# First block's output projection: from float32 products, one token tile after another, to float32r parts, half of the inner dimension at a time over all tokens

## The chip, the cores and the metric

One Trainium2 chip, one core of it. The metric is the device time of one execution of the whole program in microseconds (us), the median of repeated runs. Before the change it is 3400.55 us (three runs, 3399.44 to 3404.88).

## The reference, cut to what matters

The program is two blocks over 1024 tokens of width 1024: a state-space block, then a block with attentions and a mixture of experts. The change is in the seam between them. What is computed there, in the terms of the reference:

```python
# end of the first block: x_mix is (1024 tokens, D_INNER = 2048)
x = x + gate[:, None] * (x_mix @ w_out[i])          # w_out: 2048 x 1024
x1 = rmsnorm(x, final_norm_w)
# start of the second block
h = rmsnorm_2(x1, norm1_g[l]) * (1.0 + sc1) + sh1
proj = jnp.matmul(h, w_in[l])
```

## The kernel before, in words

`attentions` (L1838) opens a stage with `rows`, five rows of 1024 numbers broadcast over the 128 partitions (gate, final norm weight, the second block's gain and shift, and a scratch row). `second_input` (L1831) allocates `hh` and `hl` (tiles p_high and p_low), the two float32r parts of the transposed `h` that the second block's projection reads, and calls `close_first` (L1220) and then `project_second` (L1479). A float32r part pair is made so: ScalarE copies a float32 value to float32r (the high part), VectorE subtracts that from the value (the low part), and TensorE adds three products, high by high, high by low and low by high (`three`, L132).

`close_first` does not use such parts for its own product. All 16 inner slices of `w_out` (2048 x 1024, 8 MB) are brought as float32 into one tile c_w by four DMAs of 2 MB on GpSimd's queue (L1322). Then, for each tile t of 128 tokens (eight of them, `for t in range(NT)`, L1331):

- `sync(t)` (L1240) brings 128 rows of the mixer's output (2048 columns, 1 MB) into c_mix on SyncE's queue.
- `tensor_turn` (L1251) transposes them on TensorE, four 128x128 blocks a quarter, four quarters a tile, and `scalar_turn` (L1262) copies each quarter from PSUM to c_mT on ScalarE.
- `tensor(t, quarters)` (L1269) multiplies: 16 inner slices by 2 halves of 512 columns, 32 float32 products a tile, recorded through the helper `products` (L125, matmul at L128).
- `close(t)` (L1283), on VectorE: times gate (L1287), plus x (L1290), the norm's sum of squares (`Norm.rstd`, L1208), a square root on ScalarE (L1214), a reciprocal (L1216), times final norm weight giving x1 (L1295), which SyncE stores (L1297); then again a norm (L1299), gain (L1302) and shift (L1304), giving h.
- `turn_h(t)` (L1306) transposes h on TensorE in two halves (helper `turns`, L136, matmul at L138), ScalarE makes the high part (L1317), VectorE the low part (L1319).

The order on each engine is the order in which the program calls these: `tensor(t, (0, 1))`, `turn_h(t - 1)`, `tensor(t, (2,))`, two quarters of the next tile's transposes, `tensor(t, (3,))`, the other two, `close(t)`. The stage ends when all its signals have arrived; then `project_second` brings its weights (L1514), splits them into parts (L1524, L1526) and multiplies.

Of the kernel before, what the change touches and what calls it, by code (L numbers as in the profile page):

```python
# [66 lines left out]
class Stage:  # L67
# [5 lines left out]

    def sb(self, name, shape, dt=F32):
        return self.stack.enter_context(self.core.nc.sbuf_tensor(name, shape, dt))

    def sem(self, name, unit=1):
        s = self.core.nc.alloc_semaphore(name)
# [23 lines left out]
def row(ap):  # L102
    return ap.partition_broadcast(P)
# [17 lines left out]
def flat2(ap):  # L121
    return ap.rearrange("p a n -> p (a n)")
# [13 lines left out]
def turns(pe, pairs, ident):  # L136
    for o, a in pairs:
        last = pe.transpose(o, a, ident)  # L138
    return last
# [1077 lines left out]
        dve.wait_ge(*vec.now())  # L1217


def close_first(core, dram, tables, hh, hl, rows):  # L1220

    pe, dve, act, pool, sp = core.pe, core.dve, core.act, core.pool, core.sp
    ident = tables["mats"][:, C_ID, :]
    eps = tables["eps"][:, 0:1]
    with Stage(core) as s:
        KM = 2 * D // P
# [5 lines left out]
        w_in, rows_in = [s.dma(f"w_out_in{j}") for j in range(4)], s.dma("c_rows_in")  # L1232
        mix_in, x_in, turned, copied = s.pair("c_mix_in"), s.dma("c_x_in"), s.sem("c_turned"), s.sem("c_copied")
        summed, gated, added, vec, rooted = (s.sem("c_" + k) for k in ("summed", "gated", "added", "vec", "rooted"))
# [3 lines left out]
        m2 = dram["mod2"][0, :]  # L1238

        def sync(t):  # L1240
            b, at = t % 2, slice(P * t, P * t + P)
            if t >= 2:
                sp.wait_ge(*turned.at(4 * t - 4))
            sp.dma_start(mix[b][:], dram["mix"][at, :]).then_inc(*mix_in[b].up())

        def sync_x(t):
            if t:
                sp.wait_ge(*added.at(t))
            sp.dma_start(x[:], dram["x"][P * t:P * t + P, :]).then_inc(*x_in.up())

        def tensor_turn(t, quarters):  # L1251
            b = t % 2
            if quarters[0] == 0:
                pe.wait_ge(*mix_in[b].at(t // 2 + 1))
            for q in quarters:
                n = 4 * t + q
                if n >= 2:
                    pe.wait_ge(*copied.at(n - 1))
                turns(pe, [(core.bank[:, 4 + q % 2, 128 * j:128 * j + 128], mix[b][:, 512 * q + 128 * j:512 * q + 128 * j + 128])
                           for j in range(4)], ident).then_inc(*turned.up())  # L1260

        def scalar_turn(t, quarters):  # L1262
            if t >= 2:
                act.wait_ge(*summed.at(t - 1))
            for q in quarters:
                act.wait_ge(*turned.at(4 * t + q + 1))
                act.activation(mT[t % 2][:, 4 * q:4 * q + 4, :], core.bank[:, 4 + q % 2, :].rearrange("p (j n) -> p j n", j=4), ACT.Copy).then_inc(*copied.up())

        def tensor(t, quarters):  # L1269
            b = t % 2  # L1270
            if t >= 2:
                pe.wait_ge(*gated.at(t - 1))
            for q in quarters:
                if t == 0:
                    pe.wait_ge(*w_in[q].at(1))
                pe.wait_ge(*copied.at(4 * t + q + 1))
                for half in range(2):
                    last = products(pe, core.bank[:, 2 * b + half, :], [(mT[b][:, k, :], w[:, k, 512 * half:512 * half + 512])
                                                                        for k in range(4 * q, 4 * q + 4)], start=q == 0, stop=q == 3)
            if quarters[-1] == 3:  # L1280
                last.then_inc(*summed.up())

        def close(t):  # L1283
            b, at = t % 2, slice(P * t, P * t + P)
            dve.wait_ge(*summed.at(t + 1))
            dve.wait_ge(*vec.now())
            dve.tensor_tensor(y[:], flat2(core.bank[:, 2 * b:2 * b + 2, :]), gate, ALU.mult).then_inc(*gated.up())  # L1287
            dve.wait_ge(*gated.at(t + 1))
            dve.wait_ge(*x_in.at(t + 1))
            dve.tensor_tensor(y[:], y[:], x[:], ALU.add).then_inc(*added.up())  # L1290
            dve.wait_ge(*added.at(t + 1))
            norm.rstd(y[:], eps)
            if t:
                dve.wait_ge(*x1_stored.at(t))
            dve.scalar_tensor_tensor(out=x1[:], in0=y[:], scalar=norm.rs[:, 0:1], in1=fin, op0=ALU.mult, op1=ALU.mult).then_inc(*x1_done.up())  # L1295
            sp.wait_ge(*x1_done.at(t + 1))
            sp.dma_start(dram["x1"][at, :], x1[:]).then_inc(*x1_stored.up())  # L1297
            dve.wait_ge(*x1_done.at(t + 1))
            norm.rstd(x1[:], eps)  # L1299
            if t:  # L1300
                dve.wait_ge(*h_turned.at(2 * t))
            dve.scalar_tensor_tensor(out=h[:], in0=x1[:], scalar=norm.rs[:, 0:1], in1=gain, op0=ALU.mult, op1=ALU.mult).then_inc(*vec.up())  # L1302
            dve.wait_ge(*vec.now())
            dve.tensor_tensor(h[:], h[:], shift, ALU.add).then_inc(*h_done.up())  # L1304

        def turn_h(t):  # L1306
            at = slice(P * t, P * t + P)
            pe.wait_ge(*h_done.at(t + 1))
            for half in range(2):
                n, src = 2 * t + half, core.bank[:, 6 + half, :].rearrange("p (k n) -> p k n", k=4)  # L1310
                hi, lo = (a[:, 4 * half:4 * half + 4, at] for a in (hh, hl))
                if t:
                    pe.wait_ge(*h_low.at(n - 1))
                turns(pe, [(core.bank[:, 6 + half, 128 * k:128 * k + 128], h[:, 512 * half + 128 * k:512 * half + 128 * k + 128])
                           for k in range(4)], ident).then_inc(*h_turned.up())
# [5 lines left out]
        for j in range(4):  # L1321
            pool.dma_start(w[:, 4 * j:4 * j + 4, :], dram["w_out"].rearrange("(k p) n -> p k n", p=P)[:, 4 * j:4 * j + 4, :]).then_inc(*w_in[j].up())  # L1322
        sync(0), sync(1)
        for to, of in ((gate, dram["mods"][0, 2 * D:3 * D]), (fin, dram["final_norm_w"]), (gain, dram["norm1_g_2"]),
                       (tmp, m2[D:2 * D]), (shift, m2[0:D])):
            sp.dma_start(to, row(of)).then_inc(*rows_in.up())
        sync_x(0)
        dve.wait_ge(*rows_in.at(5))
        dve.scalar_tensor_tensor(out=gain, in0=tmp, scalar=1.0, in1=gain, op0=ALU.add, op1=ALU.mult).then_inc(*vec.up())
        tensor_turn(0, range(4)), scalar_turn(0, range(4))  # L1330
        for t in range(NT):  # L1331
            tensor(t, (0, 1))
            if t:
                turn_h(t - 1)
            tensor(t, (2,))
            if t + 1 < NT:
                tensor_turn(t + 1, (0, 1)), scalar_turn(t + 1, (0, 1))
            tensor(t, (3,))
            if t + 1 < NT:
                tensor_turn(t + 1, (2, 3)), scalar_turn(t + 1, (2, 3))  # L1340
            close(t)
            if t + 2 < NT:
                sync(t + 2)
            if t + 1 < NT:
                sync_x(t + 1)
        turn_h(NT - 1)


# [481 lines left out]

def second_input(core, dram, tables, rows, chosen):  # L1831
    with Stage(core) as s:
        hh, hl = (s.sb(f"p_{k}", [P, KD, SEQ], R32) for k in ("high", "low"))
        close_first(core, dram, tables, hh, hl, rows)
        project_second(core, dram, tables, hh, hl, chosen)


# [923 lines left out]
```

## Time and profile before

| | |
|---|---|
| median of three runs | 3400.55 us |
| profiled execution, its own time | 3398.51 us |
| span of the trace in it | 3396.3 us |
| granted TensorE clock, mean | 0.912 |
| TensorE busy | 2863.1 us, 84% of the span |
| VectorE busy | 2118.6 us, 62% |
| ScalarE busy | 1235.3 us, 36% |
| GpSimd busy | 535.3 us, 16% |
| DMA | 586.24 MB moved, mean 173 GB/s |

Times in the trace count from the span's start. Engines: PE is TensorE's matmul, PEld its weight load, DVE is VectorE, ACT ScalarE, POOL GpSimd, SP SyncE; a q behind the name (SPq) is an instruction that issues a DMA. A matmul's recorded duration includes its way through the array, so in a dense stream the time that one costs is the distance between two starts, not the duration. A float32 product leaves two records. The two levels of the granted clock are 1.2 and 2.4 GHz, written 0.5 and 1.0. The page's own chain of the work that ended last is empty in this profile.

### The profile page before, as it was taken

The numbers are of one execution on the slowest core, as the hardware profiler recorded it, in microseconds if no ns is written. First come the engines' busy times: TensorE is split into PE (matmuls) and PEld (weight loads), VectorE is DVE, ScalarE is ACT, GpSimd is POOL, SyncE is SP. The second block draws the span as 40 slices with busy tenths as digits, with TensorE's granted clock in tenths as the row PEclk, the third lists the DMA queues.
The fourth block names the chain that finished last, engine by engine and source line by source line (L and its number), as shares of the span: only waits on it lengthen the run. The fifth ranks groups of instructions, "written<-read, shape, count | busy, mean of one in ns | idle before, by whom it ended". The sixth has DMA issues, their size and how long they took to land.

```text
span 3396.3 us, 34380 instructions
## 1 busy us (share of the span) xinstructions
PE 2863.1 (84%) x12552; PEld 2126.6 (63%) x12552; DVE 2118.6 (62%) x2906; ACT 1235.3 (36%) x2024; POOL 535.3 (16%) x320
## 2 busy tenths in 40 slices
PE   7999959979588699879889958795988479999992
PEld 3777746755466444468767847684444368888882
DVE  6399945526688523344726979841222479999985
ACT  3122221110366511122224126572211067777772
POOL 1422100000111100001200045452110011111101
PEclk9999979989788799989999969897999689999996
DMA  6333237534455432134442164114324289999995
GB/s 204 102 103 109 88 130 257 192 127 137 164 187 177 159 135 75 44 112 119 114 122 72 72 144 89 26 41 169 117 75 157 97 316 412 416 412 414 412 389 217
DMA packets 259104, 586.24 MB, mean 173 GB/s; under 512 B 27189, under 2 KB 158245, under 8 KB 241650
## 3 DMA queue, kind: packets, MB, share of 16 engines
q1 hardware_dynamic: 185618, 449.00, 36.9%
q0 software_dynamic: 29968, 64.18, 6.4%
q10 hardware_dynamic: 43344, 70.79, 5.6%
q8 instruction: 103, 1.69, 0.2%
q14 instruction: 71, 0.58, 0.1%
HBM read 463.26 MB, written 120.65 MB: 172 GB/s over the span
## 4 chain that ended last, share of the span: by engine, by line


## 5 line engine op out<-in xcount | busy, mean ns | idle before, releaser
L2413 DVE TENSOR_TENSOR e_low<-e_raw,e_high 128x4096 fp32r<-128x4096 f32 x99 | 438.0, 4426 | 69.5 <-ACT e_high L2407 69.4
L2407 ACT ACTIVATE e_high<-e_raw 128x4096 fp32r<-128x4096 f32 x99 | 359.5, 3633 | 32.8 <-DVE live L2364 26.4
L128 PE MATMUL banks<-p_w_high,p_high 128*128 128x512 f32 (+1 forms) x640 | 250.1, 391 | 18.1 <-DVE p_w_low L1526 18.1
L128 PE MATMUL banks<-p_w_low,p_high 128*128 128x512 f32 (+1 forms) x640 | 245.8, 384 | 0.0
L128 PE MATMUL banks<-p_w_high,p_low 128*128 128x512 f32 (+1 forms) x640 | 245.1, 383 | 0.0
L128 PE MATMUL banks<-c_w,c_mT 128*128 128x512 f32 x512 | 225.9, 597 | 9.0 <-DMA c_w<-in_w_out 9.0
L128 PE MATMUL banks<-e_high,e_xhigh 128*128 128x512 f32 x528 | 211.1, 400 | 10.0 <-issue 7.2
L483 DVE SCALAR_TENSOR_TENSOR acc<-img,taps,acc 128x1024 f32<-128x1024 f32 x160 | 209.8, 1311 | 5.7
L128 PE MATMUL banks<-h_high,w_high 128*128 128x512 f32 (+1 forms) x544 | 201.0, 370 | 9.2 <-POOL w_low L355 4.5
L128 PE MATMUL banks<-e_high,e_xlow 128*128 128x512 f32 x528 | 207.9, 394 | 0.0
L128 PE MATMUL banks<-e_low,e_xhigh 128*128 128x512 f32 x528 | 207.2, 392 | 0.0
L128 PE MATMUL banks<-h_low,w_high 128*128 128x512 f32 (+1 forms) x544 | 198.2, 364 | 0.0
L128 PE MATMUL banks<-h_high,w_low 128*128 128x512 f32 (+1 forms) x544 | 198.1, 364 | 0.0
L128 PE MATMUL banks<-m_wp,m_oT 128*128 128x512 f32 x256 | 126.3, 656 | 60.7 <-DMA m_oT<-odsaT 36.0
L128 PEld LDWEIGHTS banks<-c_w,c_mT 128*128 128x128 f32 x512 | 96.5, 192 | 122.8 <-issue 113.1
L1423 DVE TENSOR_SCALAR_CACHE_REDUCE c_rows<-c_rows,i_cand 128x384 bf16<-128x384 f32 (+5 forms) x186 | 169.0, 944 | 2.2
L2544 POOL DMA_INDIRECT e_x<-h,ids x33 | 87.8, 2661 | 500.1 <-PE banks L138 458.2
L1998 POOL TENSOR_TENSOR a_P<-a_P,a_rc 128x256 f32<-128x256 f32 (+7 forms) x64 | 135.1, 2111 | 122.2 <-DVE a_rc L1990 121.6
L128 PEld LDWEIGHTS banks<-p_w_high,p_high 128*128 128x128 f32 x640 | 123.3, 193 | 40.6 <-issue 18.5
L1093 PE MATMUL banks<-s_xf,s_M 128*128 128x64 f32 x768 | 107.3, 305 | 47.9 <-DVE s_M L1050 25.4
L1093 PEld LDWEIGHTS banks<-s_xf,s_M 128*128 128x128 f32 x768 | 107.2, 222 | 59.2 <-issue 26.6
L128 PEld LDWEIGHTS banks<-p_w_high,p_low 128*128 128x128 f32 x640 | 123.1, 192 | 23.9
(452 smaller groups left out, 6127.5 us busy)
## 6 DMA issues: line engine op xcount, KB each, us to landing
e_raw<-in_exp_w SPq DMA_DIRECT2D x99, 2048.0 KB, 10.6
mod_w<-in_ada_w SPq DMA_DIRECT2D x24, 1024.0 KB, 6.1
s_sums<-cumT SPq DMA_DIRECT2D x32, 768.0 KB, 5.2
s_X<-xtok SPq DMA_DIRECT2D x19, 1024.0 KB, 7.4
p_raw<-in_w_in SPq DMA_DIRECT2D x18, 1024.0 KB, 6.5
y<-e_y ACTq DMA_DIRECT2D x33, 512.0 KB, 10.9
xbcT<-res ACTq DMA_DIRECT2D x20, 640.0 KB, 2.9
xtok<-xt ACTq DMA_DIRECT2D x20, 640.0 KB, 3.7
```

The source lines that it names most:

```text
L128: last = pe.matmul(out, a, b, start=start and n == 0, stop=stop and n == len(pairs) - 1)
L483: dve.scalar_tensor_tensor(out=grid, in0=src, scalar=wt, in1=grid, op0=ALU.mult, op1=ALU.add).then_inc(*tapped.up())
L1093: pe.matmul(core.bank[:, y0, HP * h:HP * h + HP], M[n % 2][w][:, h, :], xfs[c % 2][w][:, c0:c0 + HP], start=h == 0 and w == 0, stop=False)
L1423: dve.tensor_scalar(self.junk[n][:, 0:P * (j + 1)], self.score[j], threshold, 0.0, op, ALU.add, accum_out=count).then_inc(*self.found.up())
L1998: pool.tensor_tensor(both, both, over(rc[b][:], 2, L), ALU.mult).then_inc(*scaled.up())
L2407: act.activation(self.high[p % HIGHS][:], self.raw[p % RAWS][:], ACT.Copy).then_inc(*self.high_done.up())
L2413: dve.tensor_tensor(self.low[p % HIGHS][:], self.raw[p % RAWS][:], self.high[p % HIGHS][:].bitcast(F32), ALU.subtract).then_inc(*self.low_ ...
L2544: pool.indirect_dma_start(out=x[b][:], out_offset=None, in_=dram["h2"], in_offset=bass.IndirectOffsetOnAxis(ap=ids[:, m:m + 1].bitcast(U32 ...
```

## The change

`w_out` is used in two halves of the inner dimension (p = 0 and 1, eight slices each). A piece n is one half for one token tile: n = 0 to 7 are the eight tiles with the first half, 8 to 15 the eight tiles with the second. Both the weights and the transposed mixer output are split into float32r parts, and each product becomes three. The weights arrive as float32 in the bytes in which their low part is written later; the high part of the first half lies in `hh` and its low part in `hl`, which are free until h is transposed. The sum over the two halves is kept in SBUF: `acc` starts as x, and each piece adds gate times its product. `close` runs only in the second half. The diff, cut to its core:

```diff
@@ class Stage
+    def both(self, name, shape):
+        with self.core.nc.sbuf_tensor(name + "_raw", shape, F32) as raw:
+            pass
+        return raw, self.sb(name, shape, R32)
@@ close_first
-        w = s.sb("c_w", [P, KM, D])
+        w_raw, w_low = s.both("c_w_low", [P, KD, D])
+        raw, wh, wl = [hl_raw, w_raw], [hh, s.sb("c_w_high", [P, KD, D], R32)], [hl, w_low]
-        y, x1, h, x = (s.sb("c_" + k, [P, D]) for k in ("y", "x1", "h", "xin"))
-        mix = [s.sb(f"c_mix{b}", [P, 2 * D]) for b in range(2)]
-        mT = [s.sb(f"c_mT{b}", [P, KM, P]) for b in range(2)]
+        acc, x1 = s.sb("c_acc", [P, NT, D]), s.sb("c_x1", [P, D])
+        mix = [s.sb(f"c_mix{b}", [P, D]) for b in range(2)]
+        mh, ml = (s.sb("c_mT_" + k, [P, KD, P], R32) for k in ("high", "low"))
...
+        def load_weights(p):
+            for j in range(4):
+                pool.dma_start(raw[p][:, 2 * j:2 * j + 2, :],
+                               dram["w_out"].rearrange("(k p) n -> p k n", p=P)[:, KD * p + 2 * j:KD * p + 2 * j + 2, :]).then_inc(*w_in[p][j].up())
+
+        def split_weights(p, k):
+            act.wait_ge(*w_in[p][k // 2].at(1))
+            act.activation(wh[p][:, k, :], raw[p][:, k, :], ACT.Copy).then_inc(*w_high.up())
+            dve.wait_ge(*w_high.at(KD * p + k + 1))
+            dve.tensor_tensor(wl[p][:, k, :], raw[p][:, k, :], wh[p][:, k, :].bitcast(F32), ALU.subtract).then_inc(*w_split.up())
+
+        def sync(n):
+            p, t = n // NT, n % NT
+            if n >= 2:
+                sp.wait_ge(*turned.at(2 * n - 2))
+            sp.dma_start(mix[n % 2][:], dram["mix"][P * t:P * t + P, D * p:D * p + D]).then_inc(*mix_in[n % 2].up())
+
+        def turn(n, q):
+            m, bank = 2 * n + q, core.bank[:, 4 + q, :]
+            if q == 0:
+                pe.wait_ge(*mix_in[n % 2].at(n // 2 + 1))
+            if m >= 2:
+                pe.wait_ge(*m_low.at(m - 1))
+            turns(pe, [(bank[:, P * j:P * j + P], mix[n % 2][:, 512 * q + P * j:512 * q + P * j + P]) for j in range(4)], ident).then_inc(*turned.up())
+            act.wait_ge(*turned.at(m + 1))
+            if m >= 2:
+                act.wait_ge(*quarter.at(m - 1))
+            src, hi, lo = bank.rearrange("p (j n) -> p j n", j=4), mh[:, 4 * q:4 * q + 4, :], ml[:, 4 * q:4 * q + 4, :]
+            act.activation(hi, src, ACT.Copy).then_inc(*m_high.up())
+            dve.wait_ge(*m_high.at(m + 1))
+            dve.tensor_tensor(lo, src, hi.bitcast(F32), ALU.subtract).then_inc(*m_low.up())
+
+        def tensor(n, q):
+            p, t, b = n // NT, n % NT, n % 2
+            if q == 0 and n >= 2:
+                pe.wait_ge(*gated.at(n - 1))
+            pe.wait_ge(*m_low.at(2 * n + q + 1))
+            for k in range(4 * q, 4 * q + 4):
                 if t == 0:
+                    pe.wait_ge(*w_split.at(KD * p + k + 1))
                 for half in range(2):
+                    last = products(pe, core.bank[:, 2 * b + half, :], three(mh[:, k, :], ml[:, k, :], *(a[p][:, k, 512 * half:512 * half + 512] for a in (wh, wl))),
+                                    start=k == 0, stop=k == KD - 1)
+            last.then_inc(*quarter.up())
+
+        def gather_in(n):
+            p, t, b = n // NT, n % NT, n % 2
+            dve.wait_ge(*quarter.at(2 * n + 2))
...
+            else:
+                dve.wait_ge(*x1_stored.at(t))
+                dve.wait_ge(*vec.now())
+            dve.tensor_tensor(x1[:], flat2(core.bank[:, 2 * b:2 * b + 2, :]), gate, ALU.mult).then_inc(*gated.up())
+            dve.wait_ge(*gated.at(n + 1))
+            if p == 0:
+                dve.wait_ge(*x_in[t // 4].at(1))
+            dve.tensor_tensor(acc[:, t, :], acc[:, t, :], x1[:], ALU.add).then_inc(*added.up())
...
+        load_weights(0)
         sync(0), sync(1)
+        sp.dma_start(gate, row(dram["mods"][0, 2 * D:3 * D])).then_inc(*gate_in.up())
+        turn(0, 0), turn(0, 1)
+        for k in range(KD):
+            split_weights(0, k)
+        load_weights(1)
+        bring_x(0)
+        for n in range(PIECES):
+            p, t = n // NT, n % NT
+            tensor(n, 0)
+            if n + 1 < PIECES:
+                turn(n + 1, 0)
+            tensor(n, 1)
+            if n + 1 < PIECES:
+                turn(n + 1, 1)
+            if n + 2 < PIECES:
+                sync(n + 2)
+            if n == 1:
+                bring_x(1)
+            if n == 3:
+                bring_rows()
+            if n == 5:
+                prepare_gain()
+            if p and t:
+                turn_h(t - 1)
+            gather_in(n)
+            if p == 0:
+                split_weights(1, t)
+            else:
+                close(t)
         turn_h(NT - 1)
```

`close(t)` keeps its norms, gains and stores as they were, in place in `acc`, without the gate and the sum; `turn_h` is unchanged but for reading `acc`. `bring_x(j)` brings four token tiles of x (2 MB) into `acc` by one DMA, `bring_rows()` the four rows other than gate.

## Rows read from the trace of the kernel before

**Rows 1.** Costliest groups on the page: the stage's products and their idle time

```profile
L128 PE MATMUL banks<-c_w,c_mT 128*128 128x512 f32 x512 | 225.9, 597 | 9.0 <-DMA c_w<-in_w_out 9.0
```

**Rows 2.** A stretch of the stage: busy (count) per engine, granted clock, DMA share, GB/s

```profile
1300.00:1400.00 100.00, 100.00 (x294) 48.64 (x293) 30.98 (x39) 12.63 (x26) 0.00 (x0) 1.00 0.18 63
```

**Rows 3.** Timeline, TensorE in the middle of the stage: start, us, count

```profile
1264.25 1.04 PE L138 MATMUL banks<-mats,c_h 128*128 128x128 f32 x8
...
1265.12 7.03 PE L128 MATMUL banks<-c_w,c_mT 128*128 128x512 f32 x16
...
1294.34 1.04 PE L138 MATMUL banks<-mats,c_h 128*128 128x128 f32 x8
```

**Rows 4.** Timeline, later in the second block's projection, product of float32r parts

```profile
1462.35 0.63 PE L128 MATMUL banks<-p_w_high,p_high 128*128 128x512 f32 x1
1462.77 0.60 PE L128 MATMUL banks<-p_w_low,p_high 128*128 128x512 f32 x1
...
1463.66 0.39 PE L128 MATMUL banks<-p_w_low,p_high 128*128 128x512 f32 x1
...
1477.49 0.39 PE L128 MATMUL banks<-p_w_high,p_low 128*128 128x512 f32 x1
1477.72 0.60 PE L138 MATMUL banks<-mats,p_o 128*128 128x128 f32 x4
...
1478.39 0.39 PE L128 MATMUL banks<-p_w_low,p_high 128*128 128x512 f32 x1
```

**Rows 5.** Timeline, VectorE's close of one tile, first and last, and h's parts

```profile
1279.94 1.23 DVE L1287 TENSOR_TENSOR c_y<-banks,c_rows 128x1024 f32<-128x1024 f32 x1 [13.13 <-PE banks L128]
...
1284.25 1.28 DVE L1295 SCALAR_TENSOR_TENSOR c_x<-c_y,c_n_rs,c_rows 128x1024 f32<-128x1024 f32 x1
...
1288.68 1.22 DVE L1304 TENSOR_TENSOR c_h<-c_h,c_rows 128x1024 f32<-128x1024 f32 x1
...
1295.61 1.29 DVE L1319 TENSOR_TENSOR p_low<-banks,p_high 128x512 fp32r<-128x512 f32 x2 [5.70 <-ACT p_high L1317]
```

**Rows 6.** Groups of the projection behind it: the split of weights

```profile
L1526 DVE TENSOR_TENSOR p_w_low<-p_raw,p_w_high 128x2048 fp32r<-128x2048 f32 x4 | 9.2, 2294 | 3.0 <-ACT p_w_high L1524 3.0
L1524 ACT ACTIVATE p_w_high<-p_raw 128x2048 fp32r<-128x2048 f32 x4 | 7.7, 1916 | 0.0
```

**Rows 7.** Timeline, the start of the stage

```profile
1170.87 0.81 SPq L1244 DMA_DIRECT2D c_mix<-mix  x2
1171.62 3.24 POOL L1322 DMA_DIRECT2D c_w<-in_w_out  x4 [45.22 <-issue]
...
1172.88 0.50 SPq L1326 DMA_DIRECT2D c_rows<-in_norm_g  x1
...
1188.71 23.25 PE L128 MATMUL banks<-c_w,c_mT 128*128 128x512 f32 x48 [9.04 <-DMA c_w<-in_w_out]
...
1193.78 0.19 PEld L128 LDWEIGHTS banks<-c_w,c_mT 128*128 128x128 f32 x1 [0.30 <-issue]
```

**Rows 8.** DMA issues in the stage: count, KB each, median us to landing

```profile
c_mix<-mix SPq DMA_DIRECT2D x8, 1024.0 KB, 6.1
c_w<-in_w_out POOLq DMA_DIRECT2D x4, 2048.0 KB, 27.1
...
x<-c_x SPq DMA_DIRECT2D x8, 512.0 KB, 2.9
...
c_rows<-in_norm_g SPq DMA_DIRECT2D x1, 512.0 KB, 15.5
```

**Rows 9.** Tile c_w: its four DMAs, issue to landing

```profile
DMA to landing us min/median/max: 17.1/27.1/33.6
```

**Rows 10.** Timeline, the end of the stage

```profile
1429.53 1.23 DVE L1287 TENSOR_TENSOR c_y<-banks,c_rows 128x1024 f32<-128x1024 f32 x1 [12.26 <-PE banks L128]
...
1439.56 1.97 PE L138 MATMUL banks<-mats,c_h 128*128 128x128 f32 x8 [10.06 <-DVE c_h L1304]
...
1442.98 0.94 SPq L1514 DMA_DIRECT2D p_raw<-in_w_in  x2
```

More of the change, by code:

```diff
@@ L1217, in rstd, with close_first @@
         dve.wait_ge(*vec.now())
-def close_first(core, dram, tables, hh, hl, rows):
+def close_first(core, dram, tables, hh, hl, hl_raw, rows):
     pe, dve, act, pool, sp = core.pe, core.dve, core.act, core.pool, core.sp
@@ L1225, in close_first @@
     with Stage(core) as s:
[L1226 to L1227 removed]
+        w_raw, w_low = s.both("c_w_low", [P, KD, D])
+        raw, wh, wl = [hl_raw, w_raw], [hh, s.sb("c_w_high", [P, KD, D], R32)], [hl, w_low]
         gate, fin, gain, shift, tmp = (rows[:, k, :] for k in range(5))
[L1229 to L1234 removed]
+        acc, x1 = s.sb("c_acc", [P, NT, D]), s.sb("c_x1", [P, D])
+        mix = [s.sb(f"c_mix{b}", [P, D]) for b in range(2)]
+        mh, ml = (s.sb("c_mT_" + k, [P, KD, P], R32) for k in ("high", "low"))
+        w_in = [[s.dma(f"w_out_in{p}{j}") for j in range(4)] for p in range(2)]
+        w_high, w_split, gate_in, rows_in = s.sem("c_w_high"), s.sem("c_w_split"), s.dma("c_gate_in"), s.dma("c_rows_in")
+        mix_in, x_in, turned, m_high, m_low = s.pair("c_mix_in"), s.pair("c_x_in"), s.sem("c_turned"), s.sem("c_m_high"), s.sem("c_m_low")
+        quarter, gated, added, vec, rooted = (s.sem("c_" + k) for k in ("quarter_summed", "gated", "added", "vec", "rooted"))
         x1_done, h_done, x1_stored = s.sem("c_x1_done"), s.sem("c_h_done"), s.dma("x1_stored")
@@ L1237, in close_first @@
         norm = Norm(core, s, "c_n", vec, rooted, tmp)
[L1238 to L1273, printed above, removed]
+        m2, PIECES = dram["mod2"][0, :], 2 * NT
@@ L1274, in tensor @@
+        def tensor(n, q):
[4 more added lines that the diff above has]
+            for k in range(4 * q, 4 * q + 4):
                 if t == 0:
-                    pe.wait_ge(*w_in[q].at(1))
-                pe.wait_ge(*copied.at(4 * t + q + 1))
+                    pe.wait_ge(*w_split.at(KD * p + k + 1))
                 for half in range(2):
-                    last = products(pe, core.bank[:, 2 * b + half, :], [(mT[b][:, k, :], w[:, k, 512 * half:512 * half + 512])
-                                                                        for k in range(4 * q, 4 * q + 4)], start=q == 0, stop=q == 3)
@@ L1280, in tensor @@
-            if quarters[-1] == 3:
-                last.then_inc(*summed.up())
-        def close(t):
[L1284 to L1295, printed above, removed]
+                    last = products(pe, core.bank[:, 2 * b + half, :], three(mh[:, k, :], ml[:, k, :], *(a[p][:, k, 512 * half:512 * half + 512] for a in (wh, wl))),
+                                    start=k == 0, stop=k == KD - 1)
@@ new lines, in tensor @@
+            last.then_inc(*quarter.up())
+        def gather_in(n):
+            p, t, b = n // NT, n % NT, n % 2
+            dve.wait_ge(*quarter.at(2 * n + 2))
+            if n == 0:
+                dve.wait_ge(*gate_in.at(1))
+            elif n <= NT:
+                dve.wait_ge(*added.at(n))
+            else:
[6 more added lines that the diff above has]
+            dve.tensor_tensor(acc[:, t, :], acc[:, t, :], x1[:], ALU.add).then_inc(*added.up())
@@ L1296, in close @@
+        def close(t):
+            y = h = acc[:, t, :]
+            dve.wait_ge(*added.at(NT + t + 1))
+            norm.rstd(y, eps)
+            dve.scalar_tensor_tensor(out=x1[:], in0=y, scalar=norm.rs[:, 0:1], in1=fin, op0=ALU.mult, op1=ALU.mult).then_inc(*x1_done.up())
             sp.wait_ge(*x1_done.at(t + 1))
-            sp.dma_start(dram["x1"][at, :], x1[:]).then_inc(*x1_stored.up())
+            sp.dma_start(dram["x1"][P * t:P * t + P, :], x1[:]).then_inc(*x1_stored.up())
             dve.wait_ge(*x1_done.at(t + 1))
@@ L1299, in close @@
             norm.rstd(x1[:], eps)
-            if t:
-                dve.wait_ge(*h_turned.at(2 * t))
-            dve.scalar_tensor_tensor(out=h[:], in0=x1[:], scalar=norm.rs[:, 0:1], in1=gain, op0=ALU.mult, op1=ALU.mult).then_inc(*vec.up())
+            dve.scalar_tensor_tensor(out=h, in0=x1[:], scalar=norm.rs[:, 0:1], in1=gain, op0=ALU.mult, op1=ALU.mult).then_inc(*vec.up())
             dve.wait_ge(*vec.now())
-            dve.tensor_tensor(h[:], h[:], shift, ALU.add).then_inc(*h_done.up())
+            dve.tensor_tensor(h, h, shift, ALU.add).then_inc(*h_done.up())
@@ L1313, in turn_h @@
                     pe.wait_ge(*h_low.at(n - 1))
-                turns(pe, [(core.bank[:, 6 + half, 128 * k:128 * k + 128], h[:, 512 * half + 128 * k:512 * half + 128 * k + 128])
+                turns(pe, [(core.bank[:, 6 + half, 128 * k:128 * k + 128], acc[:, t, 512 * half + 128 * k:512 * half + 128 * k + 128])
                            for k in range(4)], ident).then_inc(*h_turned.up())
@@ L1327, in close_first, with bring_x @@
[L1327 to L1333, printed above, removed]
-                turn_h(t - 1)
[L1335 to L1345, printed above, removed]
+        def bring_x(j):
+            sp.dma_start(acc[:, 4 * j:4 * j + 4, :], dram["x"][512 * j:512 * j + 512, :].rearrange("(t p) n -> p t n", p=P)).then_inc(*x_in[j].up())
@@ new lines, in bring_rows, with prepare_gain @@
+        def bring_rows():
+            for to, of in ((fin, dram["final_norm_w"]), (gain, dram["norm1_g_2"]), (tmp, m2[D:2 * D]), (shift, m2[0:D])):
+                sp.dma_start(to, row(of)).then_inc(*rows_in.up())
+        def prepare_gain():
+            dve.wait_ge(*rows_in.at(4))
+            dve.scalar_tensor_tensor(out=gain, in0=tmp, scalar=1.0, in1=gain, op0=ALU.add, op1=ALU.mult).then_inc(*vec.up())
+        load_weights(0)
+        sync(0), sync(1)
+        sp.dma_start(gate, row(dram["mods"][0, 2 * D:3 * D])).then_inc(*gate_in.up())
@@ L1832, in second_input @@
     with Stage(core) as s:
-        hh, hl = (s.sb(f"p_{k}", [P, KD, SEQ], R32) for k in ("high", "low"))
-        close_first(core, dram, tables, hh, hl, rows)
+        hh = s.sb("p_high", [P, KD, SEQ], R32)
+        hl_raw, hl = s.both("p_low", [P, KD, SEQ])
+        close_first(core, dram, tables, hh, hl, hl_raw, rows)
         project_second(core, dram, tables, hh, hl, chosen)
```

5 lines of the change are left out of this document (removed).

## The prediction

> **What bounds the kernel now.** I read the page's costliest groups first, to find where the changed line stands: the stage's 512 records of float32 products keep TensorE busy for 225.9 us, and wait 9.0 us in all, once, for the first weights [rows 1]. Then the stage's stretch by stretch table, to see whether another engine is close: in the 100 us from 1300 on, TensorE is busy for 100.00 at granted clock 1.00, VectorE for 30.98, ScalarE for 12.63, and the DMA engines for 0.18 [rows 2]. So TensorE alone bounds this stage, which runs from its first DMA at 1170.87 to the projection's first at 1442.98 [rows 7, 10], and nothing of it overlaps with its neighbours. A microsecond taken out of it is a microsecond of the whole, until VectorE, with 9.3 us of work in each 30 us, is in the way. Last the timeline, for the price of each step.
>
> One token tile takes 30.09 us: the transposes of h start at 1264.25 and again at 1294.34 [rows 3]. Sixteen product records take 7.03 us with the last one's 0.597 in it [rows 1, 3], so two starts are (7.03 - 0.597) / 15 = 0.429 us apart, and a float32 product, two records, costs 0.858. 32 of them are 27.45; the other 2.64 are 24 transposes (16 of the mixer output, 8 of h), 0.11 each.
>
> **Part 1, three float32r products for one float32 product.** The same form, 128x128 by 512 columns of float32r parts, runs in the projection behind this stage: from the start at 1463.66 to that at 1477.49 there are 61 products, 0.2267 us each at the upper clock; at 1.2 GHz two starts lie 0.42 to 0.43 apart [rows 4]. Three cost 0.680 instead of 0.858. Over 256 products of old and 768 of new: 219.6 against 174.1, so 45.5 us less. The transposes stay 192 in number. Where four of them stand between such products, the start at 1477.49 is followed by two products' worth and the transposes until 1478.39: 0.90, less 0.45, makes 0.45 for four [rows 4], the same 0.11 each. The Trainium skill prices a product lower (TensorE: Matmul & The Clock Gate, section "Back-to-back issue gap": 518 cycles for 512 columns at the upper clock, 0.216 us). By it the 768 would take 165.8 us and the sum would come out 8 us lower; the row has 0.2267 and the sum goes by the row.
>
> So TensorE's time for a piece is 48 x 0.2267 + 8 x 0.11 = 11.76 us in the first half, and with eight transposes of h 12.65 us in the second.
>
> **Part 2, VectorE's new work.** In the first half a piece has two low parts of the transposed mixer output (1.29 for two) [rows 5], gate and sum (2.52), and one slice of weights to split. A split of 2048 columns takes 2.294, one of 1024 about 1.23, as any 128x1024 operation of VectorE here [rows 5, 6]. Together 5.1 of 11.76: hidden. ScalarE has two high parts of 0.6 and a split of about 1.06 (half of 1.916 and its fixed part): hidden too.
>
> In the second half `close` comes with every piece. From the gate to the shift it takes 1279.94 to 1289.90, 9.96 us [rows 5]; two low parts of h and two of the next piece are 2.58: 12.54 us of 12.65. Nothing is left to hide behind, so the order counts. The loop is: shift of tile t ends; TensorE, which waits at `turn_h(t)`, transposes; high and low parts follow; only then, being behind them on VectorE, `gather_in` and `close` of the next piece. From the first transpose to the end of the second low part it is 1294.34 to 1296.90, 2.56 [rows 3, 5], and with 9.96 and two hand-overs of about 0.05 a round is 12.6. The low parts of the next piece fall into the gap in which TensorE and ScalarE work on h. TensorE's round and this one are equal within a tenth; I take 12.68 for pieces 10 to 14. If the two low parts do not fit into the gap, a round is 1.29 longer, over seven rounds 9 us: the upper end. The lower end is TensorE's own 12.65.
>
> **Part 3, waits added.** `gather_in` writes x1, so in the second half it waits for the previous store of x1. The store is issued when x1 is ready, 5.6 us after the gate began [rows 5], and lands after 2.9 [rows 8]; the next gate begins 12.68 after the last, so 7.1 are there for some 3.3: nothing. Behind this wait would stand all of `close`. On SyncE's queue a piece's mixer rows stand behind that store; they are issued some 10 us before TensorE wants them, half the size of what landed in 6.1 before [rows 8]: nothing. x for four tiles (2 MB), twice, and four rows (2 MB) go out while the DMA engines are at 0.18: nothing, and without this cover piece 4 would wait for its x.
>
> **Part 4, the start.** Before, the first product started at 1188.71, when the first 2 MB of weights had landed, and ran at the lower clock until 1193.78 [rows 7]. After, the first piece needs 4 MB of weights, each slice split. Up to 1172.88 SyncE's queue had issued 3.5 MB (two mixer tiles, three rows); the last of these landed 15.5 later, at 1188.4 [rows 7, 8]. The new kernel issues 3.5 MB there too (two half tiles, gate, x for four tiles), so 2 MB of weights should again be there at about 1188.7. The other three quarters landed up to 33.6 after issue, 1205 to 1208 [rows 9]: 6 MB in some 17 to 19 us with 1.5 MB of SyncE's, 0.4 MB a us. So 4 MB are there at about 1193.5. Behind them: a copy (1.06), two subtractions (2.46) and the last slice's six products (1.4): 1198.4. The clock is the open term. In the old kernel it rose after 5 us of unbroken work; with work that comes slice by slice it may rise only after 1196, and then the second half of the piece ends near 1202; wholly at 1.2 GHz it ends near 1206. I take 1200.5, with 1197 and 1206 as ends.
>
> **Part 5, the end.** The last product record ended about 1429.5 and the stage 13.45 later [rows 10]. After, `gather_in(15)` stands behind h's parts of tile 6, which TensorE may start only 0.8 after its last product (piece 15 has no next piece, 12.23 long): 0.8 + 2.5 more. So 16.7.
>
> **Sum.** From 1200.5, nine pieces of 11.76 (n = 1 to 9; tile 0's h is first turned behind piece 9) are 105.8, five of 12.68 are 63.4, one of 12.2, and the end 16.7: 1398.6. Before it was 1442.98: 44.4 us less. The profiled execution took 3398.51, 2.04 less than the median of the runs and 2.2 more than its span, so it would become 3354.1, and the median 3356.2. Before has no cover to lose elsewhere: the projection behind starts from its own first DMA, as now.
>
> **Rivals.**
> 1. VectorE becomes the bound in the second half: its 12.54 of work do not pack, the round is 14 to 14.5 us. For it: the two loads are equal to a tenth, and each part of h passes three engines. Against: the gap behind h's transposes is there. 9 to 13 us lost: 3366 to 3370. Chance 0.15.
> 2. The start is better than I think and products go at less than 0.2267: 3345 to 3349. Chance 0.06.
> 3. Slower than before: short stops of TensorE in each piece bring the clock down. Stops of VectorE's making come in every round of the second half, and the clock did fall in the trace when TensorE stood still (it was 1.2 GHz at 1188.71 and in the last transposes, 1.97 for eight instead of 1.04 [rows 3, 7, 10]). At the lower clock 48 products take 20.5 and 16 transposes 3.9: 24.4 a piece instead of 12.65, so eight pieces lose 94 us and the kernel ends at 3450. It decides from about four pieces on: each gives away 11.8, and 44.4 are there. The Trainium skill has this as a rule against such a loop (the same page, section "HAM oscillation — how this bites in real kernels": repeated waits put the clock down again every round). In the trace only stops of about 10 us before [rows 10] are seen with it, and here a stop should be under 1 us. Chance 0.04.
> 4. The change does not do what it says: the three products, or the written-over weights, bring a wait at each slice, and the stage stays as long as it was (within 7 us). The same form runs densely in the projection [rows 4], against it. Chance 0.03.
>
> **How the numbers follow.** The forecast, 3356.2, has 0.72, with its own range from 3349 (start at 1197, rounds of 12.65, and some of rival 2) to 3364 (start at 1206, and part of the low parts exposed). The range over the cases takes in rival 1 nearly whole and the lower rival: 3346 to 3370. A measurement of this kernel tells 0.2%, 6.8 us, from no change. Faster by more: forecast, rivals 1 and 2, 0.93; within: 0.03; slower: 0.04.
>
> **What would show it.** In the profile after, product starts 0.227 apart with granted clock 1.00 from about 1200 to the end of the stage; two transposes of h 11.8 apart at first and then 12.7; the projection's first DMA near 1399 instead of 1442.98; VectorE busy nearly without a gap from about 1305 on, above 90%. Wrong would be: VectorE's gate waiting for the store of x1; rounds over 13.5; granted clock 0.5 anywhere between 1210 and 1380; or the first split waiting for weights beyond 1195.

## The result, and the profile after

| | before | after |
|---|---|---|
| median | 3400.63 us (3399.44 to 3404.88, four runs) | 3360.89 us (3357.5 to 3364.0, four runs) |
| ratio after / before | | 0.9881, interval 0.9864 to 0.9898 |
| span of the trace | 3396.3 us | 3355.8 us |
| the stage, from its first DMA to the projection's first | 1170.87 to 1442.98: 272.1 us | 1172.41 to 1402.43: 230.0 us |

The median is 39.7 us lower. The forecast was 44.4 lower, 3356.2, with a range of 3346 to 3370. In the traces the stage is 42.1 us shorter. It begins 1.5 us later, in code that the change does not touch, and from the projection's first DMA to the end of the span it is 1953.3 us before and 1953.4 after: nothing is lost or gained behind.

The stretches of the stage after the change. Columns: stretch, its length, busy us and (count) of PE, PEld, DVE, ACT and POOL, granted clock, DMA share, GB/s:

```profile
1172.00:1188.00 16.00, 2.17 (x9) 1.82 (x10) 2.96 (x4) 3.20 (x4) 5.95 (x8) 0.50 0.90 324
1188.00:1203.00 15.00, 13.53 (x52) 10.50 (x53) 8.43 (x8) 6.50 (x7) 0.00 (x0) 0.88 1.03 410
1203.00:1297.00 94.00, 94.00 (x446) 77.74 (x445) 40.15 (x41) 17.16 (x24) 0.00 (x0) 1.00 0.29 103
1297.00:1385.00 88.00, 88.00 (x439) 73.56 (x438) 76.86 (x101) 17.09 (x39) 0.00 (x0) 1.00 0.21 72
1385.00:1404.00 19.00, 3.83 (x20) 2.74 (x18) 12.99 (x17) 2.87 (x6) 0.00 (x0) 0.62 0.10 31
```

TensorE still has no gap from 1203 to 1385, at granted clock 1.00 (before: [rows 2]). VectorE is the new thing to see: it is busy for 76.86 of 88 us in the second half, where it had 31 of 100.

The start, from the timeline (start, us, engine):

```profile
1172.41 0.81 SPq L1265 DMA_DIRECT2D c_mix<-mix  x2
1187.78 0.77 PE L134 MATMUL banks<-p_high,c_mT_high 128*128 128x512 f32 x1 [8.83 <-DVE p_low L1258]
1191.70 0.39 PE L134 MATMUL banks<-p_high,c_mT_high 128*128 128x512 f32 x1
1195.04 2.00 ACT L1256 ACTIVATE p_high<-p_low_raw 128x1024 fp32r<-128x1024 f32 x2 [2.41 <-DMA p_low_raw<-in_w_out]
1197.38 2.01 ACT L1256 ACTIVATE p_high<-p_low_raw 128x1024 fp32r<-128x1024 f32 x2 [0.34 <-DMA p_low_raw<-in_w_out]
1197.51 0.47 PE L134 MATMUL banks<-p_high,c_mT_high 128*128 128x512 f32 x1 [1.04 <-DVE p_low L1258]
1203.05 0.60 PE L144 MATMUL banks<-mats,c_mix 128*128 128x128 f32 x4
```

The first half's weights come in four pairs of slices. The last pair is there 25.0 us after the stage's start (the prediction had 22.6), the clock is up at 1191.70 (the prediction had left open whether it would be before 1196), and the first piece's products end at 1203.05, 30.65 after the start, where 29.6 were forecast. TensorE's last wait in this piece is for the third pair: it is copied from 1195.04 on, its products start at 1197.51, and from there TensorE has no gap. These lines answer to [rows 7].

One round of the second half, from the timelines of VectorE and TensorE:

```profile
1308.43 1.22 DVE L1323 TENSOR_TENSOR c_acc<-c_acc,c_rows 128x1024 f32<-128x1024 f32 x1
1309.58 0.68 DVE L1280 TENSOR_TENSOR c_mT_low<-banks,c_mT_high 128x512 fp32r<-128x512 f32 x1
1310.94 0.69 DVE L1280 TENSOR_TENSOR c_mT_low<-banks,c_mT_high 128x512 fp32r<-128x512 f32 x1 [0.68 <-ACT c_mT_high L1278]
1311.55 1.28 DVE L1338 TENSOR_TENSOR p_low<-banks,p_high 128x512 fp32r<-128x512 f32 x2
1312.74 1.22 DVE L1306 TENSOR_TENSOR c_x<-banks,c_rows 128x1024 f32<-128x1024 f32 x1
...
1321.48 1.22 DVE L1323 TENSOR_TENSOR c_acc<-c_acc,c_rows 128x1024 f32<-128x1024 f32 x1
```

```profile
1309.67 0.60 PE L144 MATMUL banks<-mats,c_mix 128*128 128x128 f32 x4
1310.11 1.04 PE L144 MATMUL banks<-mats,c_acc 128*128 128x128 f32 x8
1316.48 0.60 PE L144 MATMUL banks<-mats,c_mix 128*128 128x128 f32 x4
1322.41 0.60 PE L144 MATMUL banks<-mats,c_mix 128*128 128x128 f32 x4
1322.85 1.04 PE L144 MATMUL banks<-mats,c_acc 128*128 128x128 f32 x8
```

The shift of tile 0 ends at 1309.65, and TensorE is free to transpose it at 1310.11: VectorE arrives 0.46 us before it is needed, and in the next round (shift from 1321.48 to 1322.70, transposes at 1322.85) 0.15 before. A round, from one transposing of h to the next, is 12.74 us (1310.11 to 1322.85). With its first-half piece of 11.85 us a tile takes 24.6, against 30.09 in [rows 3]. The two low parts of the next piece and h's own two fall into the gap between shift and gate, as forecast (1309.58 to 1312.8).

The end answers to [rows 10]:

```profile
1385.39 0.39 PE L134 MATMUL banks<-c_w_high,c_mT_low 128*128 128x512 f32 x1
1386.46 1.09 PE L144 MATMUL banks<-mats,c_acc 128*128 128x128 f32 x8 [0.69 <-DVE c_acc L1323]
1388.99 1.22 DVE L1306 TENSOR_TENSOR c_x<-banks,c_rows 128x1024 f32<-128x1024 f32 x1
...
1402.43 0.94 SPq L1550 DMA_DIRECT2D p_raw<-in_w_in  x2
```

The last product starts at 1385.39 and gives way 0.23 later (when the next could start), 16.8 us before the projection's first DMA. From the end of its record, as the 13.45 of before is counted, it is 16.65.

### The profile page after: what moved, and what is told of

It is laid out like the page before. It is cut to its first block, busy times and chain, and to the rows that moved or that the text cites. A ratio compares the mean times of both kernels' runs of the same rounds, so it can differ in the third digit from the quotient of the medians.

```text
span 3355.8 us, 35015 instructions
## 1 busy us (share of the span) xinstructions
PE 2817.8 (84%) x12808; PEld 2169.3 (65%) x12808; DVE 2181.5 (65%) x2970; ACT 1249.9 (37%) x2040; POOL 538.1 (16%) x324
## 4 chain that ended last, share of the span: by engine, by line
## 5 line engine op out<-in xcount | busy, mean ns | idle before, releaser
L134 PEld LDWEIGHTS banks<-p_w_low,p_high 128*128 128x128 f32 x640 | 123.6, 193 | 21.8
L134 PEld LDWEIGHTS banks<-m_wp,m_oT 128*128 128x128 f32 x256 | 53.8, 214 | 128.3 <-issue 92.6
```

Source lines behind the costliest of these rows:

```text
L134: last = pe.matmul(out, a, b, start=start and n == 0, stop=stop and n == len(pairs) - 1)
```

## Experiments

Ten kernels were run. As the time up to the stage's start scatters between traces of equal code (below), the lengths of the stage and of its rounds are read from the traces, to a tenth, and the times of whole runs serve only where they differ by more.

### Float32 products in the new order

```diff
-                    last = products(pe, ..., three(mh[:, k, :], ml[:, k, :], *(... for a in (wh, wl))), ...)
+                    last = products(pe, ..., [(mh[:, k, :], raw[p][:, k, 512 * half:512 * half + 512])], ...)
-        for k in range(KD):
-            split_weights(0, k)
-            if p == 0:
-                split_weights(1, t)
```

`mh` is float32 here, and no low part is made.

> The changed kernel with its order kept (halves of the inner dimension, sum in SBUF) but its products in float32 again, and no split of weights or of the mixer output. Theory (the whole gain is TensorE's cheaper products): a piece takes 16 x 0.858 + 8 x 0.11 = 14.6 us in the first half and 15.5 in the second, TensorE without a wait; with about 30 for the first piece and 16 for the end the stage lasts about 270 us against 230 changed and 272 before; time 3395 to 3402. Rival (the new order, with x, weights and rows brought apart from each other, carries part of the gain): stage 250 to 260, time 3380 to 3390.

3397.84 us, one run, beside 3397.26 of before on the same chip. The stage is 1174.00 to 1443.08, 269.1 us. Two stretches, one in each half, and two starts of h's transposes:

```profile
1208.00:1320.00 112.00, 112.00 (x307) 52.48 (x306) 18.29 (x15) 8.96 (x15) 0.00 (x0) 1.00 0.21 73
1320.00:1425.00 105.00, 105.00 (x320) 51.97 (x319) 70.39 (x89) 17.19 (x39) 0.00 (x0) 1.00 0.18 60
```

```profile
1335.14 1.04 PE L144 MATMUL banks<-mats,c_acc 128*128 128x128 f32 x8
...
1350.63 1.04 PE L144 MATMUL banks<-mats,c_acc 128*128 128x128 f32 x8
```

15.49 us a round, 15.5 expected. The new order alone is worth 3 us of stage, the float32r products, with all their splitting, 39.1. The theory holds.

### One product of three

```diff
-three(mh[:, k, :], ml[:, k, :], *(...))
+three(mh[:, k, :], ml[:, k, :], *(...))[0:1]
```

> Leaves out two of the three products (high by low and low by high); all splits, copies and sums stay. TensorE's own work for a piece falls from 11.8 to 4.5 us (first half) and from 12.7 to 5.4 (second). Theory (in the second half VectorE's loop is as long as TensorE's): the rounds of the second half stay at 12.6 to 12.7 and only the first half shrinks, to VectorE's 5.2 to 5.6 a piece; stage about 177 us, 53 less than changed; time 3302 to 3312. Rival (VectorE has room in the second half, its loop packs shorter): rounds of 11 or less in the second half, stage below 165, time below 3297.

3313.39 us; stage 1175.28 to 1356.84, 181.6 us, where about 177 were expected. The first half went as expected, 5.2 us a piece. The second half stayed at VectorE's length, but its rounds are 13.26, longer than the changed kernel's 12.74 with three times the products:

```profile
1245.00:1340.00 95.00, 52.52 (x225) 43.00 (x223) 82.35 (x106) 18.31 (x40) 0.00 (x0) 0.78 0.20 70
```

```profile
1287.12 1.97 PE L144 MATMUL banks<-mats,c_acc 128*128 128x128 f32 x8 [6.17 <-DVE c_acc L1323]
...
1300.38 1.97 PE L144 MATMUL banks<-mats,c_acc 128*128 128x128 f32 x8 [6.00 <-DVE c_acc L1323]
```

The rival, room on VectorE, is out. The theory's 12.6 to 12.7 missed by 0.6: TensorE stands still for some 6 us a round, the granted clock is 0.78 in the mean, and the transposes of h, which stand in VectorE's loop, take 1.97 us for eight instead of 1.04 to 1.09.

### Two products of three

```diff
+three(mh[:, k, :], ml[:, k, :], *(...))[0:2]
```

> Leaves out the low by high product alone. TensorE's work in a second-half round falls from 12.74 to 9.1 us, its stops are half as long as with one product. Theory (VectorE's loop is 12.4 to 12.5 at the upper clock, as the run with one more VectorE operation gives, 13.68 less 1.24; with one product it was 13.26 because eight transposes of h at the lower clock stand in it, 1.97 us instead of 1.09): rounds 12.4 to 12.5 if the granted clock is 1.00 there, 13.2 to 13.3 if it is 0.5 at the transposes; first-half pieces 8.1 to 8.3, TensorE's. Rival (the loop of VectorE is really 13.2 and the changed kernel's TensorE hides part of it): 13.2 at clock 1.00.

3327.36 us, stage 1173.17 to 1373.00, 199.8 us. This kernel has rounds of both lengths. The transposes of h start at 1279.93, 1292.47, 1305.02, 1318.28, 1331.23, 1343.78, 1356.32 and 1369.58, so the rounds are 12.54, 12.55, 13.26, 12.95, 12.55, 12.54 and 13.26. Both rounds of 13.26 begin with transposes that took 1.97 us, the one of 12.95 with 1.67, the other four with 1.09. A fast and a slow one:

```profile
1279.93 1.09 PE L144 MATMUL banks<-mats,c_acc 128*128 128x128 f32 x8 [3.07 <-DVE c_acc L1323]
...
1305.02 1.97 PE L144 MATMUL banks<-mats,c_acc 128*128 128x128 f32 x8 [3.23 <-DVE c_acc L1323]
```

So VectorE's loop is 12.55 us with TensorE at the upper clock and 13.26 with it at the lower one, and the changed kernel's TensorE, at 12.74, binds by 0.2. The stop before the transposes does not settle alone which it is: they were slow behind stops of 3.23, 2.38 and 4.17 us, and not behind one of 3.07. The first-half pieces took 8.22, as expected.

### One more VectorE operation a round

```diff
+            dve.tensor_tensor(tmp, x1[:], gate, ALU.mult)
             dve.tensor_tensor(h, h, shift, ALU.add).then_inc(*h_done.up())
```

> One more VectorE operation of 128x1024 (1.22 us, its output is not used) ahead of each shift, in the second half only; nothing on TensorE. Theory (VectorE's loop and TensorE's are equal, VectorE's idle 1.1 us a round are waits within its loop): rounds go from 12.74 to 13.8 to 14.0, stage 7.5 to 9.5 longer: time 3363 to 3366. Rival (TensorE alone bounds the second half, VectorE's work is hidden): rounds stay at 12.74 and only the end grows, by 1.2: time 3357.

3366.03 us, stage 1177.40 to 1414.38, 237.0 us: 7.0 more, a little under the 7.5 expected. Its first piece, which the edit does not touch, ended 0.7 earlier after the start (29.95 against 30.65); behind it 7.65 were added. The rounds are 13.68, and TensorE waits in each:

```profile
1315.18 1.09 PE L144 MATMUL banks<-mats,c_acc 128*128 128x128 f32 x8 [0.58 <-DVE c_acc L1324]
...
1328.86 1.09 PE L144 MATMUL banks<-mats,c_acc 128*128 128x128 f32 x8 [0.75 <-DVE c_acc L1324]
...
1342.55 1.09 PE L144 MATMUL banks<-mats,c_acc 128*128 128x128 f32 x8 [0.74 <-DVE c_acc L1324]
```

1.24 us were added and 0.94 came through a round, less than the 1.06 to 1.26 expected: VectorE had 0.3 to spare by this run and 0.2 by the one before. "Hidden" is out. Stops of 0.75 us a round did not bring the clock down: the transposes of h took 1.09 in each round.

### x after the first weights

```diff
         load_weights(1)
+        sp.wait_ge(*w_in[0][3].at(1))
         bring_x(0)
```

> SyncE issues the first 2 MB of x only when the last of the first 4 MB of weights has landed. Theory (the first piece is paced by the arrival of its weights, which share the DMA engines with x): the weights land 4 to 5 us earlier, about 20 after the stage's start instead of 24.9, the first piece's products end 26 to 27 after it instead of 30.65, and the stage is 3.5 to 5 shorter: time 3351 to 3353. VectorE's first sum waits for x, without harm to TensorE. Rival (the queue of GpSimd sets the pace of the weights, not the share): first piece as before, time 3356 or above.

3363.0 us, stage 1178.02 to 1408.4, 230.4 us. The first piece's products ended at 1203.55, 25.5 us after the start, a little better than the 26 to 27 of the theory and 5.1 earlier than in the changed kernel; but nothing of this arrived at the end. SyncE's queue and TensorE's transposes show where it went:

```profile
1195.78 0.38 SPq L1341 DMA_DIRECT2D c_acc<-in_x  x1
1196.21 8.29 SPq L1265 DMA_DIRECT2D c_mix<-mix  x2
```

```profile
1203.55 0.60 PE L144 MATMUL banks<-mats,c_mix 128*128 128x128 f32 x4
1213.34 0.66 PE L144 MATMUL banks<-mats,c_mix 128*128 128x128 f32 x4 [3.70 <-DMA c_mix<-mix]
```

The mixer rows of piece 2, which the changed kernel issues at 1178.98, 6.6 us into its stage, stand on SyncE's queue behind the added wait and went out 18.2 us in, behind 2 MB of x. TensorE waited 3.7 us for them in piece 1, and the stop brought its clock down: eight products behind it start 0.43 apart, and the half piece from 1213.34 to 1220.91 takes 7.57 us instead of 5.92. The wait (3.9 from transposes to transposes) and the clock (1.65) together are 5.5, which is the 5.1 won and the 0.4 by which the stage is longer. The expectation had looked at VectorE's wait for x and not at what is queued behind a wait on SyncE.

### The same, behind the mixer rows

```diff
         load_weights(1)
-        bring_x(0)
...
             if n + 2 < PIECES:
                 sync(n + 2)
+            if n == 0:
+                sp.wait_ge(*w_in[0][3].at(1))
+                bring_x(0)
```

> The late x of the earlier run again, but the wait and x's transfer stand on SyncE's queue behind the mixer rows of piece 2. There the rows had stood behind the wait and TensorE got them late: piece 1's first transposes came 9.8 us after piece 0's last instead of 5.9. Theory (that queueing took back all of the gain): no such gap, the first piece ends 26 to 27 after the start, and the stage is 225 to 226.5 us instead of 230.0. Rival (the late x itself holds VectorE and through it TensorE): the gap stays, stage 229 or more.

3358.95 us; stage 1176.71 to 1402.15, 225.4 us: 4.6 less. The first piece ends 25.8 after the start and the gap is gone:

```profile
1183.38 0.32 SPq L1265 DMA_DIRECT2D c_mix<-mix  x1
1196.12 0.38 SPq L1341 DMA_DIRECT2D c_acc<-in_x  x1
```

```profile
1196.58 0.60 PE L144 MATMUL banks<-mats,c_mix 128*128 128x128 f32 x4
1202.49 0.60 PE L144 MATMUL banks<-mats,c_mix 128*128 128x128 f32 x4
```

So the first piece is paced by its weights sharing the DMA engines with x. The rival, late x holding TensorE through VectorE, is out.

### The clock brought up before the first weights

```diff
         turn(0, 0), turn(0, 1)
+        turns(pe, [(core.bank[:, 6, 128 * (j % 4):128 * (j % 4) + 128], ident) for j in range(56)], ident)
```

> The changed kernel with 56 more transposes of the identity into an unused bank right behind the first mixer transposes, about 9 us of TensorE work, so that the granted clock is at its upper level when the first weights are split. Theory (the first piece is paced by the arrival of its weights, and the nine products at the lower clock cost nothing): the first piece's products end 30.3 to 30.9 after the stage's start as now (30.65), stage 229.7 to 230.3. Rival (the open clock term of the prediction's fourth part is real, 1.8 us or more): they end at 28.8 or earlier.

3360.64 us, stage 1172.54 to 1402.58, 230.0 us. The added work ends at 1186.5 and the first products start 0.23 apart, at the upper clock:

```profile
1187.54 0.47 PE L134 MATMUL banks<-p_high,c_mT_high 128*128 128x512 f32 x1 [1.04 <-DVE p_low L1258]
1187.85 0.39 PE L134 MATMUL banks<-p_low,c_mT_high 128*128 128x512 f32 x1
```

The first piece's products end at 1203.31, 30.8 after the start. The clock term that the prediction left open is worth nothing here, since the products wait for weights in any case: the third pair is copied from 1195.31 on, 22.8 after the start (22.6 in the changed kernel), and the piece ends 8.0 later in both.

### The last gate and sum ahead of h's parts

```diff
-            if p and t:
+            if p and t and n + 1 < PIECES:
                 turn_h(t - 1)
             gather_in(n)
+            if n + 1 == PIECES:
+                turn_h(t - 1)
```

> For the last piece alone, VectorE takes gate and sum before the two low parts of the h of tile 6, not behind them. Theory (the extra of the end, 16.8 us instead of 13.45, is the wait for h's parts standing ahead of the last gate): from the last product to the projection's first DMA 15.4 to 15.6 us instead of 16.8, the stage 1.3 shorter, 228.7. Rival (the end is VectorE's work alone, whatever its order): 16.8.

3359.55 us, stage 1177.45 to 1405.12, 227.7 us. Its first piece came 0.7 earlier than the changed kernel's (29.97 after the start), as in the run with one more VectorE operation, with no edit there. The end is 15.2 us (the last product gives way at 1389.89) where it was 16.8 and 15.4 to 15.6 were expected, so 1.6 of the 2.3 belong to the edit:

```profile
1389.47 1.22 DVE L1323 TENSOR_TENSOR c_acc<-c_acc,c_rows 128x1024 f32<-128x1024 f32 x1
...
1390.62 1.22 DVE L1306 TENSOR_TENSOR c_x<-banks,c_rows 128x1024 f32<-128x1024 f32 x1
...
1393.01 1.28 DVE L1338 TENSOR_TENSOR p_low<-banks,p_high 128x512 fp32r<-128x512 f32 x2
```

### The changed kernel again, and all three edits together

The second of these has the late x, the last sum first and 44 added transposes.

> The changed kernel as it is, for a comparison on the same chip as the next one, and to see which part of the scatter between runs lies in the stage. Theory (the stage is 42 us shorter and nothing else moves): stage 229.5 to 230.5 us again, ratio to before 0.9860 to 0.9885, and the time up to the stage's start differs between traces of equal code by some us. Rival (part of the 39.7 us measured was gained or lost outside of the stage): stage as before, ratio outside of these bounds.

> x behind the mixer rows and the first weights, the last gate and sum ahead of the h parts of tile 6, and 44 added transposes that bring the clock up before the first weights. Theory (the two gains of 4.5 and 1.6 us add up, and with the weights 7 us earlier the first piece is now partly paced by TensorE, so the clock is worth 1 to 1.6 more where it was worth nothing before): first piece's products end 24.2 to 24.9 after the start, stage 222.3 to 223.5 us, 7 less than the changed kernel: time 3350 to 3356, ratio to before 0.984 to 0.986. Rival (the clock stays worth nothing): first piece at 25.8, stage 224.

| | median of four | ratio to before | stage |
|---|---|---|---|
| changed kernel again | 3362.11 us | 0.9885, interval 0.9869 to 0.9902 | 1171.46 to 1401.32: 229.9 us |
| the three edits | 3350.15 us | 0.9853, interval 0.9836 to 0.9870 | 1171.56 to 1394.76: 223.2 us |

The stage of the changed kernel is 229.9 and 230.0 us in its two traces; the two ratios agree. The three edits make it 6.7 shorter, as expected, and the whole interval of their ratio lies below 1. Against the changed kernel the medians stand 12 us apart, more than the stage can account for, and the two intervals touch; what is shown is the stage.

One expectation failed: the first piece should have ended at 24.2 to 24.9 with the clock up, and ended at 25.5. From the trace:

```profile
1185.89 2.00 ACT L1256 ACTIVATE p_high<-p_low_raw 128x1024 fp32r<-128x1024 f32 x2 [2.26 <-DMA p_low_raw<-in_w_out]
...
1188.27 0.50 PE L134 MATMUL banks<-p_high,c_mT_high 128*128 128x512 f32 x1 [1.18 <-DVE p_low L1258]
1191.17 0.60 PE L144 MATMUL banks<-mats,c_mix 128*128 128x128 f32 x4
1197.08 0.60 PE L144 MATMUL banks<-mats,c_mix 128*128 128x128 f32 x4
```

The second pair of weights lands 14.3 us after the start, its products start 2.4 later, and from there TensorE has no gap. A fast start in the first pair ends in a wait for the second.

## Why the prediction was right

**Part 1, the products.** Right, and the whole of the gain: with float32 products in the new order the stage is 269.1 us, with float32r parts 230.0. The sum had 45.5 less TensorE work; that is 2.84 a piece. Against the float32 run the fifteen pieces behind the first are 2.76 shorter each, 41.4 together; the first piece, paced by its weights, ends 1.4 later after the stage's start, and the end is 0.9 longer: 39.1 remain. Between starts 0.2267 us is what the trace shows in the middle of each group; the first eight or so products behind a group of transposes stand up to 0.24 apart (the first 0.31), which makes a first-half piece 11.85 us instead of 11.76 (from 1203.05 to 1297.83 there are eight). Over nine pieces this is 0.8 us. The 0.216 us that the prediction cites (the Trainium skill, TensorE: Matmul & The Clock Gate, section "Back-to-back issue gap") is in that section the gap of a matmul by itself; for a stream with weight loads it has about 131 ns at 512 columns. Neither is reached here: the changed kernel's dense products, a weight load before each, stand 0.2267 us apart, and the measurement decides.

**Part 2, VectorE.** Right in its main point, that both loops are equal to a few tenths, and in the packing: measured 12.74 for TensorE (12.65 and 12.68 were the figures) and 12.55 for VectorE's loop (12.6). Rival 1, a loop of 14 us, did not come; the two low parts lie in the gap.

**Part 3, added waits.** None shows: in the waits of VectorE between 1297 and 1385 stand only 5.1 us for ScalarE's roots and 7.8 for its high parts, none for a DMA:

```profile
DVE c_mT_low L1280 <- ACT c_mT_high L1278: 7.8, 7, 5.2
DVE c_n_rs L1222 <- ACT c_n_sd L1220: 5.1, 14, 0.4
```

**Part 4, the start.** 1.0 us too short, which is partly luck: three errors, two of which add up and one of which takes back.

- The last pair of weights came 25.0 instead of 22.6 us after the start. Half of the 4 MB was there at 18.2, close to the 17.8 forecast. For the other half the sum gave all of the engines' 0.4 MB a us to it. The rate is right (408 GB/s from 1190.6 to 1197.4), but in these 6.8 us GpSimd's queue moved 2.39 MB, of which the pairs are 2.10, and SyncE's 0.38. By these rates the 0.67 MB of others take 1.6 us and the pairs' own 2.10 MB 5.1 instead of 4.8; with the 0.4 of the first half this is 2.3 us.
- Behind the last pair the sum has 4.9 us, for a copy, two subtractions and six products. But the wait that ends last is for the third pair, and behind it stand 24 products: from the start of its copy to the end of the piece it is 8.0 us in all five traces that bring weights and x in this order and make all three products, whether the piece ends 29.95 or 30.8 after the start. From the last pair it is 5.7 here, 0.8 more than the sum has.
- The clock, for which 2.1 us had been added and which set the ends of the range of 9 us, was worth 0.

2.3 and 0.8 less 2.1 are the 1.0.

**Part 5, the end.** 16.7 forecast, 16.8 measured; with the order changed it is 15.2.

The misses add up: 1.0 at the start, 0.8 in nine pieces, 0.3 in five rounds and 0.2 in the last piece and the end, 2.3 us: the stage is 42.1 shorter instead of 44.4. The other 2.4 us between 42.1 and the 39.7 of the medians lie outside the stage, where traces of equal code differ by more (last section). That the measured median lies 4.7 us from the forecast is thus in half a matter of this scatter.

Of the signs that the prediction names, the distances, the clock and the waits for stores came as it says. The projection's first DMA is at 1402.43 instead of near 1399, 1.5 us of which is the later start. VectorE is busy for 71.42 of the 80 us from 1305, 89% and not above 90, and weights of the first half were waited for until 1197.38, beyond its 1195.

**The rival on the other side**, the clock falling in each round of the second half, did not happen: granted clock 1.00 from 1203 to 1385. The run with two products shows how near such a state is: with stops of 1.6 to 4.2 us a round the clock fell in some rounds, and with 0.75, in the run with one more VectorE operation, in none. In the run with late x a single stop of 3.7 us brought it down. The Trainium skill's rule (same page, section "HAM oscillation — how this bites in real kernels") is thus borne out by the run with one product, whose transposes of h took 1.97 us in every round, behind stops of 4.8 to 6.7 us, and does not apply to this change.

## What to carry to other kernels

Float32r parts pay where TensorE alone binds, at 0.680 for 0.858 us here; before counting on it, add up what the splitting does to the engine that closes each tile, since 12.55 us of VectorE's loop beside 12.74 of TensorE's means that the next cut in TensorE's work in the second half brings only 0.2 us a round. Before a wait is put on a queue, list what stands behind it there: the same 5 us were won and lost again by the place of one transfer. And at a stage's start bring first what TensorE needs first: 2 MB of x beside 4 MB of weights cost 4.6 us.

## What was not expected of the hardware

- Less work on TensorE made the second half slower per round: 13.26 us with one product of three, 12.74 with all three. The transposes in the loop took 1.97 instead of 1.09 us at the lower clock, behind stops of some 6 us. The run with two products has both lengths of round in one kernel, with slow and fast transposes.
- The time from the program's start to this stage's first DMA, in twelve traces with equal code up to there, lies between 1170.87 and 1178.02 us, while the changed kernel's stage was 230.0 and 229.9 us in its two traces, and 230.0 with the added transposes. It does not always repeat so well: in two other traces with the same start the first piece ended 0.7 earlier, because the third pair of weights landed earlier. What makes the 7 us and the 0.7 is open. A change of a few us is read better from a stage than from the whole time, and one of less than 1 us only from the part of the stage that it touches.
